# Gate tiles of two attention mixers handed out in halves, with an accumulator bank of their own

## The reference, cut to what matters

```python
z = rmsnorm(x, norm1_g[l]) @ w_in[l]
z_mla, z_nsa, z_fox, z_dsa, z_gate = split_cols(z, [...])
o_mla, o_nsa, o_fox, o_dsa = ...            # latent, sparse-block, forgetting, indexed attention
branches = jnp.stack([o_mla, o_nsa, o_fox, o_dsa], axis=2)
lifted = jnp.einsum('bsnc,ncd->bsnd', branches, w_branch[l])
gates = jax.nn.sigmoid(z_gate.reshape(B, S, N_BRANCH, D_MODEL))
mixed = jnp.sum(gates * lifted, axis=2)
x = x + mixed @ w_out[l]
h2 = rmsnorm(x, norm2_g[l])
x = x + jnp.square(jax.nn.relu(h2 @ w_up[l])) @ w_down[l]
```

## Time and profile before

| | |
|---|---|
| median of 3 runs | 1809.6 us (1806.76 to 1813.25) |
| the profiled execution | 1817.32 us, its span 1815.5 us |
| mean granted TensorE clock | 0.949 |
| TensorE busy (matmul) | 1660.4 us, 91% of the span |
| VectorE, ScalarE, GpSimd busy | 807.5, 727.5, 516.5 us |
| mixers of layer 0: W1, W2, W3 with the tail | 853.5 to 933, to 1006.6, to 1068.5 us |

### The profile page before, as it was taken

The page is one execution under the profiler, slowest core; times in us unless marked ns, Lnnn a source line. Parts: engine busy times, 40 slices in busy tenths (PEclk is TensorE's granted clock), DMA queues, the critical chain, the costliest instruction groups (busy, mean ns, idle before and its releaser), DMA issues.

```text
span 1815.5 us, 24507 instructions
## 1 busy us (share of the span) xinstructions
PE 1660.4 (91%) x10218; PEld 1405.8 (77%) x10218; DVE 807.5 (44%) x1508; ACT 727.5 (40%) x1044; POOL 516.5 (28%) x182
## 2 busy tenths in 40 slices
PE   5999979998897999979999878999899998779997
PEld 4756867787896778868888667999788886669996
DVE  3623578634666884353252453222432432632321
ACT  3324367533336674342123343444422223344441
POOL 1200035431001453342000045655530000455554
PEclk8979889999998999989899998999998999989999
DMA  9568279865625897423433143555443332325550
GB/s 387 206 210 292 85 275 345 307 256 205 222 92 203 298 333 297 161 83 106 147 122 140 47 143 116 190 190 178 151 142 116 127 143 70 116 96 199 191 189 34
DMA packets 46654, 327.33 MB, mean 180 GB/s; under 512 B 5456, under 2 KB 5456, under 8 KB 8784
## 3 DMA queue, kind: packets, MB, share of 16 engines
q1 hardware_dynamic: 46544, 325.76, 50.1%
HBM read 324.69 MB, written 1.05 MB: 179 GB/s over the span
## 4 chain that ended last, share of the span: by engine, by line
PE 77%; DVE 14%; ACT 4%; DMA 2%; POOL 2%; issue 1%; DVEq 0%; SPq 0%; ACTq 0%; POOLq 0%
PE ps L201 27%; PE ps L204 16%; PE ps L206 15%; PE ps L205 15%; DVE lo L212 5%; DMA raw<-in_wmod 2%; ACT hi L209 1%; POOL lo L212 1%; DVE xn L212 1%; PE ps L2502 1%; DVE ar L212 1%; DVE hTl L212 1%; DVE gl L212 1%; ACT ar L209 1%; DVE big L220 1%
## 5 line engine op out<-in xcount | busy, mean ns | idle before, releaser
L212 POOL TENSOR_TENSOR lo<-raw,hi 128x2048 fp32r<-128x2048 f32 (+2 forms) x92 | 425.8, 4639 | 671.0 <-ACT hi L209 671.0
L209 ACT ACTIVATE hi<-raw 128x2048 fp32r<-128x2048 f32 (+2 forms) x216 | 396.0, 1863 | 33.9 <-PE ps L206 17.8
L212 DVE TENSOR_TENSOR lo<-raw,hi 128x2048 fp32r<-128x2048 f32 (+1 forms) x124 | 338.0, 2743 | 119.1 <-ACT hi L209 119.1
L201 PE MATMUL ps<-hT,raw 128*128 128x256 f32 x1024 | 235.5, 387 | 0.0
L201 PEld LDWEIGHTS ps<-hT,raw 128*128 128x128 f32 x1024 | 194.3, 193 | 30.8 <-issue 3.6
L204 PE MATMUL ps<-hTh,hi 128*128 128x256 f32 x640 | 184.1, 288 | 10.9 <-DVE lo L212 6.1
L206 PE MATMUL ps<-hTh,lo 128*128 128x256 f32 x640 | 183.1, 286 | 0.0
L205 PE MATMUL ps<-hTl,hi 128*128 128x256 f32 x640 | 182.9, 286 | 0.0
L204 PE MATMUL ps<-hi,gh 128*128 128x512 f32 x320 | 131.7, 412 | 16.1 <-DVE lo L212 16.1
L204 PEld LDWEIGHTS ps<-hTh,hi 128*128 128x128 f32 x640 | 124.8, 195 | 12.5 <-DVE lo L212 6.6
L204 PE MATMUL ps<-hi,hTh 128*128 128x512 f32 (+3 forms) x320 | 118.8, 371 | 16.6 <-DVE hTl L212 10.5
(11 more groups left out here) (284 smaller groups left out, 2736.9 us busy)
## 6 DMA issues: line engine op xcount, KB each, us to landing
raw<-in_wgu SPq DMA_DIRECT2D x64, 1024.0 KB, 4.9
raw<-in_wmod SPq DMA_DIRECT2D x48, 1024.0 KB, 5.7
raw<-in_wdn SPq DMA_DIRECT2D x32, 1024.0 KB, 5.0
raw<-in_wgt SPq DMA_DIRECT2D x32, 1024.0 KB, 4.9
raw<-in_wup SPq DMA_DIRECT2D x32, 1024.0 KB, 4.8
raw<-in_wdown SPq DMA_DIRECT2D x32, 1024.0 KB, 5.3
raw<-in_wz SPq DMA_DIRECT2D x12, 1024.0 KB, 4.9
raw<-in_wbr SPq DMA_DIRECT2D x8, 1024.0 KB, 6.9
```

What stands on the lines that cost most here:

```text
L201: return self.e.matmul(o, l, r, start=first, stop=last)
L209: return self.e.activation(o, a, f, **kw)
L212: return self.e.tensor_tensor(o, a, b, op)
```

## The change

A gate tile is handed out in two steps: four matmuls, a yield, four matmuls. In W1 the filler is called twice a turn (`both`), so that a turn still gets a whole tile; in W2 and W3 a turn gets half a tile. ScalarE's filler has an empty step ahead of each tanh, VectorE's and GpSimd's have 64 empty steps instead of 32. Pool F (bank 4 alone) serves the gates, pool M (banks 5 to 7) all else of the mixers that was in B; B itself stays for the rest of the program.

```diff
-        self.turn = dict(A=0, B=0, G=0, C=0, S=0)
+        self.turn = dict(A=0, B=0, G=0, C=0, S=0, F=0, M=0)
...
-    POOLS = dict(A=(0, 4), B=(4, 4), G=(4, 2), C=(6, 2), S=(0, 3))
+    POOLS = dict(A=(0, 4), B=(4, 4), G=(4, 2), C=(6, 2), S=(0, 3), F=(4, 1), M=(5, 3))
...
-                b = t.take("B", "gate", l, d, n)
+                b = t.take("F", "gate", l, d, n)
                 t.wait_ge(*t.at("landed", c.key))
                 t.wait_ge(*t.free(b))
                 for k in range(8):
                     m = t.mm(self.ps[:, b, 0:256], wv[:, k, 128 * (n % 2):128 * (n % 2) + 128], self.hT[:, k, :],
                              k == 0, k == 7)
+                    if k == 3:
+                        yield
                 m.then_inc(*t.up(f"full{b}"))
                 t.mark("used", c.key)
                 yield
...
-                b = t.take("B", "lift", l, n, d)
+                b = t.take("M", "lift", l, n, d)
...
         a.wait_ge(*a.at("used", ("z", l, 5, 1)))
         for d in range(8):
             for n in range(4):
+                yield
                 b = a.bank("gate", l, d, n)
                 a.wait_ge(*a.full("gate", l, d, n))
                 a.ac(V.sg[:, n, d, :], self.ps[:, b, 0:256], ACT.Tanh, scale=0.5).then_inc(*a.up(f"free{b}"))
...
     def v_fill(self, v, l):
         V = self.views2()
-        for d in range(8):
-            for n in range(4):
-                yield
+        for _ in range(64):
+            yield
...
     def t_mixers(self, t, l):
...
         step = lambda: next(fill, None)
+        both = lambda: (step(), step())
...
         for _ in self.t_heads(t, l):
-            step()
-        weave([self.t_indexer(t, l), self.t_compress(t, l)], 2, step)
+            both()
+        weave([self.t_indexer(t, l), self.t_compress(t, l)], 2, both)
```

More of the change, by code:

```diff
@@ L2138, in t_indexer @@
         V, ps = self.views2(), self.ps
-        b = t.take("B", "idx q", l)
+        b = t.take("M", "idx q", l)
         t.wait_ge(*t.at("idx rope", l))
@@ L2146, in t_indexer @@
         m.then_inc(*t.up(f"full{b}"))
-        b = t.take("B", "idx k", l)
+        b = t.take("M", "idx k", l)
         t.wait_ge(*t.at("idx keys", l))
@@ L2259, in t_heads @@
         for i, c0 in enumerate((0, 128, 448, 576)):
-            b = t.take("B", "hq", l, i)
+            b = t.take("M", "hq", l, i)
             t.wait_ge(*t.at("rope", l))
@@ L2266, in t_heads @@
         for i in range(3):
-            b = t.take("B", "hk", l, i)
+            b = t.take("M", "hk", l, i)
             t.wait_ge(*t.at("doubled", l, i))
@@ L2317, in t_compress @@
         w2 = [t.chunk("cmp", l, s) for s in range(2)]
-        b = t.take("B", "cmp in", l)
+        b = t.take("M", "cmp in", l)
         t.wait_ge(*t.at("rope", l))
@@ L2326, in t_compress @@
         yield
-        b = t.take("B", "cmp", l)
+        b = t.take("M", "cmp", l)
         t.wait_ge(*t.at("windows", l))
@@ L2337, in t_compress @@
         yield
-        b = t.take("B", "cmp kv", l)
+        b = t.take("M", "cmp kv", l)
         t.wait_ge(*t.empty("cmp", l))
@@ L2344, in t_compress @@
         yield
-        b = t.take("B", "cmp k", l)
+        b = t.take("M", "cmp k", l)
         t.wait_ge(*t.empty("cmp kv", l))
@@ L2362, in t_compress @@
         for q in range(2):
-            b = t.take("B", "cmp p", l, q)
+            b = t.take("M", "cmp p", l, q)
             t.wait_ge(*t.at("cmp prob", l))
@@ L2497, in t_attend @@
             for kt in range(i + 1):
-                b = t.take("B", "prob T", l, name, i, kt)
+                b = t.take("M", "prob T", l, name, i, kt)
                 t.wait_ge(*t.at("prob", l, name, i))
@@ L2581, in t_values @@
     def t_values(self, t, l, n, paths, ready):
-        b = t.take("B", "branch", l, n)
+        b = t.take("M", "branch", l, n)
         t.wait_ge(*t.free(b))
@@ L2617, in t_latent @@
         for i in range(3):
-            b = t.take("B", "cT", l, i)
+            b = t.take("M", "cT", l, i)
             t.wait_ge(*t.at("latent", l))
@@ L2626, in t_latent @@
         for q in range(2):
-            b = t.take("B", "mla q", l, q)
+            b = t.take("M", "mla q", l, q)
             t.wait_ge(*t.empty("cT", l, 2))
@@ L2633, in t_latent @@
             m.then_inc(*t.up(f"full{b}"))
-            b = t.take("B", "mla kv", l, q)
+            b = t.take("M", "mla kv", l, q)
             t.wait_ge(*t.free(b))
@@ L2641, in t_latent @@
             for hp in range(2):
-                b = t.take("B", "mla T", l, c0, hp)
+                b = t.take("M", "mla T", l, c0, hp)
                 t.wait_ge(*t.at("mla rope", l))
@@ L2723, in t_forget @@
         yield
-        b = t.take("B", "decay", l)
+        b = t.take("M", "decay", l)
         t.wait_ge(*t.at("log f", l))
@@ L2731, in t_forget @@
             for s in range(2):
-                b = t.take("B", "fox T", l, q, s)
+                b = t.take("M", "fox T", l, q, s)
                 t.wait_ge(*t.at("fox in", l, q))
@@ L2847, in a_mixers @@
         step = lambda: next(fill, None)
+        both = lambda: (step(), step())
         for _ in self.a_heads(a, l):
             a.mark("kk", l)
-            step()
-        weave([self.a_indexer(a, l), self.a_compress(a, l)], 2, step)
+            both()
+        weave([self.a_indexer(a, l), self.a_compress(a, l)], 2, both)
         def latent():
@@ L2872, in v_mixers @@
         step = lambda: next(fill, None)
+        both = lambda: (step(), step())
         for _ in self.v_heads(v, l):
-            step()
-        weave([self.v_indexer(v, l), self.v_compress(v, l)], 2, step)
+            both()
+        weave([self.v_indexer(v, l), self.v_compress(v, l)], 2, both)
         weave([self.v_attend(v, l, "nsel", 0.125, self.causal, V.sgl[:, :, 4:8]),
@@ L2892, in g_mixers @@
         step = lambda: next(fill, None)
+        both = lambda: (step(), step())
         wait = lambda n: (None for _ in range(n))
         for _ in self.g_heads(g, l):
-            step()
-        weave([wait(11), self.g_compress(g, l)], 2, step)
+            both()
+        weave([wait(11), self.g_compress(g, l)], 2, both)
         weave([self.g_attend(), self.g_attend(lambda: g.lifts.append(1)), wait(3)], 3, step)
```

## The result

The changed kernel took 1819.2 us (median of 20 runs, 1805.2 to 1828.2 but for one disturbed run of 3278.6, which the comparison leaves out), the kernel before 1811.2 us (20 runs, 1801.6 to 1813.9) beside it on the same chip. The ratio is 1.0054 with an interval of 1.0037 to 1.0071, that is 9.8 us slower (6.7 to 12.9). Forecast were 6.7 us, 1816.3.

A forecast was written before the change was run, and what follows sets the result against it. TensorE was taken to bound the kernel. New waits of 17.5 us a layer (35.0) less 28.3 of idle time and lost clock removed gave +6.7 us, so 1816.3 us, 0.4% slower, range about 1811 to 1823.

The forecast's parts named there:

- The mechanism: Mixers of both layers: 28.3 us of idle time and lost clock removed, 35.0 of new waits added, net +6.7.
- The short reuse: A gate tile's first matmul waits until ScalarE empties the single bank: 0.70 us each, bounds 0.58 to 0.90.
- The stalls behind exps: In the attention weaves, gate tiles wait for a tanh queued behind exps: four stalls a layer, 1.7 to 1.9 us each.
- The packed input: Forget attention, last weave: TensorE waits 1.2 us for VectorE's packed input, in place of 2.03.
- the last transposes of the sparse attention: In the last weave these transposes wait 0.8 us, against 0.98 before the change.
- I expect no half clock: Last weave: no stretch at granted clock 0.50, so the 2.9 and 1.6 us lost there before are won.
- some 17: The last weave, with its tail of lifts, becomes some 17 us longer.
- The tail and the DMAs at nothing: Ten lifts of 1.73 us with GpSimd keeping pace, output product waiting as now, and weight loads costing nothing.
- Level out: Whole kernel: gains equal losses, reuse costing 2.6 us less and exp stalls 3.2 less: 1810.5 us; chance 0.23.
- Tanhs not behind exps: Attention weaves: ScalarE reaches the tanh in time, four large stalls go, 7.1 us a layer: 1802 us; chance 0.13.
- Clock in the new gaps: Short gaps in the first two weaves lower the clock: 1850 us, or 1825 at two tiles a layer; chance 0.07.
- Three banks too few: At some four places of the last weave, transposes or lifts wait 0.3 to 1 us: 1821 us; chance 0.05.

The follow-up runs named there:

- the kernel with the tanh first: The changed kernel, but ScalarE takes the tanh of four gate tiles a layer a step earlier, ahead of the exps: 1804.4 us, 0.9975 of before.
- two-and-two kernel: The changed kernel, but with two banks for the gates and two for all else of the mixers: 1797.0 us, 0.9936 of before.

## Why the prediction was right, point by point

**The mechanism.** Right: the halves and the bank pull in opposite directions, and the bank wins. Alone they are worth -19.9 and +25.5 us. The size is right with some luck: against the forecast's sum W1 cost 0.6 us more and W3's stalls 1.2 us less in the two layers, and a half clock that had been ruled out added 1.7, together +1.1, which is the mixers' 7.8 for the forecast 6.7.

**The short reuse.** Taken at 0.70 us (0.58 to 0.90); measured from start to start 0.67 to 0.78. W1 grew by 5.9 and 5.8 us (5.8 and 5.8 without the narrow part) where 5.5 were forecast, the heads by 0.32 where 0.3 were. Sharing the banks in W1 took the whole of it away, and no other edit was in that kernel: shown.

**The stalls behind exps.** Right in place and in size. W2 has waits of 1.47 and 1.57 us in brackets where 1.7 each were forecast, and two of 0.47 where 0.70 were taken, but these brackets start at modelled ends:

```profile
946.54 1.99 PE L201 MATMUL ps<-hT,raw 128*128 128x256 f32 x8
...
972.19 1.14 PE L201 MATMUL ps<-ar 64*128 64x256 f32 x8
974.90 1.96 PE L201 MATMUL ps<-hT,raw 128*128 128x256 f32 x8 [1.57 <-ACT big L209]
```

From start to start the half at 946.54 takes 3.47 us up to 950.01, 1.74 more than the usual 1.73, and the scores at 972.19 take 2.71, 1.65 more than the 1.06 that the same scores take ahead of them (969.20 to 970.26). With two short ones of 0.67 and 0.64 and a smaller one of 0.30 (958.39, four transposes in 0.73 us where 0.43 is usual) W2's stalls sum to 5.0 us, as forecast. It is 20.9 us shorter; 21 were forecast. W3's two are 1.71 and 1.97 from start to start (1.54 and 1.81 in brackets) for the forecast 1.9 and 1.85:

```profile
997.01 1.89 PE L201 MATMUL ps<-hT,raw 128*128 128x256 f32 x8
1000.45 3.72 PE L201 MATMUL ps<-hT,raw 128*128 128x256 f32 x16 [1.54 <-ACT big L209]
...
1005.76 1.06 PE L2737 MATMUL ps<-cst,s 128*66 128x128 f32 x8 [1.03 <-DVE s L232]
...
1016.62 1.05 PE L201 MATMUL ps<-ff 66*128 66x128 f32 x8
1019.48 5.38 PE L201 MATMUL ps<-hT,raw 128*128 128x256 f32 x16 [1.81 <-ACT big L209]
...
1055.07 1.09 PE L2503 MATMUL ps<-cst,ar 128*128 128x128 f32 x8 [0.24 <-DVE ar L212]
```

The packed input is late by 1.03 (1.2 forecast) and the last transposes of the sparse attention by 0.24 (0.8 forecast): they had been walked through without the time that VectorE gains at the stalls ahead of them, which would explain it, though no run here tries that alone. The idle time of W3 is 5.3 us by modelled ends where 6.7 were forecast. From start to start it is about 6.1: W3 of layer 1 takes 4.7 us more than with shared banks, where it idles 1.4. That 4.7 is also what the forecast had for its four stalls at gate tiles; the 0.6 too many are the packed input and the transposes. That the long stalls need the order on ScalarE beside the single bank is shown by the kernel with the tanh first, in which they shrink to 0.47.

**The step that failed: "I expect no half clock".** The row at 1019.48 above is a gate tile that took 5.38 us; rows at full clock take 3.7. The next tile starts 5.85 us behind it, in layer 1 4.16: 1.7 us lost. The granted clock of that stretch, and of the same place in layer 1:

```profile
1019.40:1024.90 5.50, 5.38 (x16) 4.10 (x16) 2.01 (x3) 1.48 (x9) 0.00 (x0) 0.69 0.28 116
1535.50:1539.20 3.70, 3.67 (x16) 2.96 (x16) 1.96 (x3) 1.42 (x8) 0.00 (x0) 1.00 0.37 153
```

The same program, with the same row of stalls, fell to half clock in one layer and not in the other; with W1 shared it fell in both. The stretch I had relied on, 16.6 us at 1.00 with 3.1 us of idle in it, showed that such idle need not bring the clock down, not that it can't. What decides between the layers stays open: the runs show the stall of 1.81 us ahead of each fall and the same stall without one. W3 grew by 18.9 and 18.4 us. The text's "some 17" was rounded too low: its own terms (7.5 tiles of 3.46 us, 6.7 us of stalls, less the old idle time and lost clock) make 18.0 and 19.1. With 0.6 us less of stalls, and 1.7 at half clock in layer 0, that is 19.1 and 18.4, against the measured 18.9 and 18.4.

**The tail and the DMAs at nothing.** Right. The ten lifts run without a wait, 17.53 us for 80 matmuls, and the output product waits 5.27 us, as before (5.26). No wait for weights is new in the mixers:

```profile
1059.32 17.53 PE L201 MATMUL ps<-oTs,raw 128*128 128x256 f32 x80
1082.12 0.76 PE L204 MATMUL ps<-hi,hTh 128*128 128x512 f32 x1 [5.27 <-DVE hTl L212]
```

**The rivals.** *Level out*: the forecast differences of 2.6 and 3.2 us did not come; the ratio's interval, from 1.0037 up, excludes it. *Tanhs not behind exps*: excluded by the rows of ScalarE. *Clock in the new gaps*: W1 of layer 0 shows the same granted clock as before, 0.94 (all of it lost in the narrow part; from 890.7 us on it is 1.00), though eight of its tiles now stand behind short waits, and W2, with four waits of 0.47 to 1.57 us, stands at 1.00. The Trainium skill, TensorE: Matmul & The Clock Gate, section "A second HAM failure mode: psum-queue depth-cycling", by which the clock swings when short idles come of turning through banks, isn't borne out in this fp32 kernel for the ten idles of 0.35 to 0.56 us in W1 and W2 of layer 0; the one fall came behind a stall of 1.81 us, in one layer of two. *Three banks too few*: in the changed kernel only the heads' 0.32 us, which the forecast had (its W2 and W3 have no such wait), but it appears as soon as the tanh stalls go (1.36 us), and with two banks it is 1.68.

## What to carry to other kernels

Splitting a rotation of buffers by purpose takes slack from both sides: here, in the order of before, four shared banks show no wait in W1 and W2 and one plus three cost 18.7 us in the mixers. A producer with a single buffer runs at the pace of its consumer's queue, so look at what stands ahead of the emptying instruction in that queue, and count the reuses with nothing between them. The Trainium skill, Perfetto Trace Analysis, section "Identifying Performance Opportunities", says that the same gap repeated on the engine that should be saturated can mean too few buffers; the 31 waits on one pair in the list above, 22 of them of 0.35 to 0.56 us in the mixers, are that picture.

When a change has two parts, cost them apart. Filler spread evenly over the phases that starve was worth 1% here, and hardly depended on halving it; the change paid that and more for a bank that it didn't need.

## What the runs showed of the hardware that was not expected

A gate tile behind the 1.81 us stall showed a granted clock of 0.69 over 5.5 us in three of four layers looked at (one of two in the changed kernel, both with W1 shared), with the same instructions ahead of it. In the two-and-two kernel the last lift, behind 7.5 us of idle time, took 3.2 us at a granted clock of 0.50, where a lift at full clock takes 1.75 (17.53 for ten), and the output product started at once behind it, its first 5.6 us at 0.96; in the changed kernel, where the idle time stands right ahead of the output product, that product's first 5.9 us are granted 0.51:

```profile
1063.20:1066.40 3.20, 3.20 (x8) 2.57 (x9) 2.35 (x4) 0.63 (x1) 0.00 (x0) 0.50 0.00 0
...
1066.40:1072.00 5.60, 5.60 (x25) 4.63 (x24) 3.00 (x5) 2.33 (x3) 0.00 (x0) 0.96 0.72 262
```

```profile
1082.10:1088.00 5.90, 5.88 (x14) 4.34 (x15) 4.30 (x7) 1.26 (x2) 0.00 (x0) 0.51 0.64 271
```

The lost clock goes to whatever stands first behind the idle time. Worked out from the granted clock it is 1.8 us in the two-and-two kernel (1.6 in the lift, 0.2 behind it) and 2.9 in the changed kernel. That this is a saving isn't shown: in layer 1 the same places give 1.8 (0.50 over 3.3 us, 0.97 over 5.8) and 1.7 (0.71 over 5.9).
